# The first norm and modulation of a decoder layer, in four groups by feature chunk

## What is computed

```python
mod = silu(c) @ ada_w + ada_b          # shift1, scale1, gate1, shift2, ... per sequence
h = rmsnorm(x, g1) * (1 + scale1) + shift1
p = h @ w_in                           # queries, keys, values, mLSTM and pool inputs
```

## Time and profile before

| | us |
|---|---|
| three runs of the kernel before | 932.52, 932.40, 927.18; median 932.4 |
| profiled execution, its own time | 932.81 |
| its span in the profile | 931.0 |
| TensorE busy (matmuls) | 845.6 (91%) |
| VectorE, ScalarE, GpSimd busy | 494.6, 348.5, 337.8 |
| chain that ended last | TensorE 73%, of it the product line L687 56% |

### The profile page before, as it was taken

The page is one execution under the profiler, slowest core; times in us unless marked ns, Lnnn a source line. Parts: engine busy times, 40 slices in busy tenths (PEclk is TensorE's granted clock), DMA queues, the critical chain, the costliest instruction groups (busy, mean ns, idle before and its releaser), DMA issues.

```text
span 931.0 us, 19070 instructions
## 1 busy us (share of the span) xinstructions
PE 845.6 (91%) x7555; PEld 750.2 (81%) x7555; DVE 494.6 (53%) x938; ACT 348.5 (37%) x675; POOL 337.8 (36%) x204
## 2 busy tenths in 40 slices
PE   4669999998998688899899699999999999999994
PEld 3458999987556564566699599999999999999994
DVE  0061456565435985667547756666621366667224
ACT  2432222233322133656432355555311355554321
POOL 0133455451000584434324134444344444443440
PEclk9869999999555655999989899999999999999998
DMA  9732788883105772445026123434322333222222
GB/s 346 289 131 73 221 265 261 270 261 129 35 13 179 283 269 41 105 116 154 8 79 254 46 80 114 114 113 115 102 92 91 106 113 121 93 92 90 92 63 92
DMA packets 72438, 128.28 MB, mean 138 GB/s; under 512 B 13652, under 2 KB 48156, under 8 KB 72096
## 3 DMA queue, kind: packets, MB, share of 16 engines
q1 hardware_dynamic: 65664, 109.65, 36.9%
q10 hardware_dynamic: 6656, 17.43, 5.6%
q0 software_dynamic: 32, 0.00, 0.0%
HBM read 121.39 MB, written 9.11 MB: 140 GB/s over the span
## 4 chain that ended last, share of the span: by engine, by line
PE 73%; DVE 13%; SPq 7%; issue 2%; ACT 2%; DMA 1%; POOL 0%; DVEq 0%; ACTq 0%; POOLq 0%
PE ps L687 56%; SPq L490 2%; PE ps L855 2%; PE ps L870 2%; SPq L429 2%; PE ps L744 2%; PE ps L943 1%; PE ps L922 1%; PE ps L907 1%; DVE sq L1354 1%; PE ps L957 1%; SPq L516 1%; DMA arena<-cache_keys 1%; PE ps L737 1%; DVE hR L1362 1%
## 5 line engine op out<-in xcount | busy, mean ns | idle before, releaser
L687 PE MATMUL ps<-hR,wR 128*128 128x260 f32 x3504 | 436.4, 286 | 21.7 <-ACT hR L1051 17.8
L687 PEld LDWEIGHTS ps<-hR,wR 128*128 128x128 f32 x3504 | 429.9, 191 | 27.1 <-issue 19.3
L641 POOL TENSOR_TENSOR wR<-raw,wR 128x1024 fp32r<-128x1024 f32 x95 | 227.7, 2397 | 321.8 <-ACT wR L1043 321.8
L1043 ACT ACTIVATE wR<-raw 128x1024 fp32r<-128x1024 f32 x95 | 100.4, 1058 | 217.8 <-PE ps L687 214.2
L687 PE MATMUL ps<-fR,wR 128*128 128x260 f32 x1056 | 128.1, 283 | 2.2 <-DVE fR L1746 2.0
L687 PEld LDWEIGHTS ps<-fR,wR 128*128 128x128 f32 x1056 | 127.0, 188 | 3.1 <-DVE fR L1746 2.4
L1768 DVE COPY arena<-arena 128x2 f32<-128x2 f32 x44 | 47.1, 1071 | 94.1 <-ACT arena L1301 94.1
L578 POOL TENSOR_TENSOR arena<-arena,par 128x1024 f32<-128x1024 f32 x16 | 33.4, 2089 | 89.8 <-DMA arena<-cache_keys 89.8
L1372 DVE TENSOR_REDUCE arena<-arena 128x64 f32<-128x1024 f32 x16 | 19.5, 1219 | 86.0 <-POOL arena L578 86.0
L1731 DVE TENSOR_TENSOR t<-ps,mod 128x8 f32<-128x8 f32 x24 | 4.0, 166 | 108.8 <-PE ps L687 108.8
L635 POOL TENSOR_SCALAR arena<-arena,fac 128x128 f32<-128x128 f32 (+3 forms) x32 | 40.7, 1274 | 57.2 <-DVE fac L1685 57.1
(11 more groups left out here) (334 smaller groups left out, 994.6 us busy)
## 6 DMA issues: line engine op xcount, KB each, us to landing
raw<-weights SPq DMA_DIRECT2D x95, 512.0 KB, 3.8
arena<-cache_keys SPq DMA_DIRECT2D x128, 192.0 KB, 3.3
arena<-weights SPq DMA_DIRECT2D x24, 512.0 KB, 10.5
arena<-cache_values SPq DMA_DIRECT2D x128, 64.0 KB, 1.9
arena<-weights ACTq DMA_DIRECT2D x12, 512.0 KB, 5.6
raw<-weights ACTq DMA_DIRECT2D x12, 512.0 KB, 4.8
x<-xT SPq DMA_DIRECT2D x8, 260.0 KB, 6.3
out_y<-x SPq DMA_DIRECT2D x8, 260.0 KB, 2.2
```

What stands on the lines that cost most here:

```text
L641: nc.gpsimd.tensor_tensor(wR[:, i % 2, 1, :, :], raw[:, g % RAW, :, :], wR[:, i % 2, 0, :, :].bitcast(F32), ALU.subtract).then_inc(lo_read ...
L687: last = mm(ps[:, a + half, 0:TH], wR[:, i % 2, wp, k, :], src[:, hp, j, half * TH:(half + 1) * TH], start=(j == 0 and q == 0), stop=(j == ...
L1043: A(wR[:, i % 2, 0, :, :], raw[:, g % RAW, :, :], ACT.Identity).then_inc(hi_ready, 1)
```

## The change

The 16 modulation items are reordered into four groups; group c holds scale and shift of feature chunks 2c and 2c+1. A group's four items go through TensorE in one go into one PSUM bank, through ScalarE in one copy (`group_read`), and through one set of four turns. Bias, `ab`, sample columns, normings and both halves of hR are then made for two feature chunks at a time. The first two projection items, 16 and 17, run chunk by chunk beside each other between the groups. The squares are added on VectorE, as in the other two norms, and TensorE sums the total once. Slots 16 and 17 are loaded ahead of slots 8 to 15. SyncE waits for two groups before it loads the first cache half, since slots 2 to 7 now lie there. `half_sums(0)` comes behind the norm, `value_products(0)` behind the first two low halves.

```diff
-EARLY_GROUP = [0, 1, 2, 2, 3, 3, 3, 3, 4, 4, 4, 4, 5, 5, 5, 5]
+EARLY_GROUP = [i // 4 for i in range(EARLY)]
...
-    part1 = [("ada", t, KD) for t in range(16)] + [("in", t, KD) for t in range(N_IN)]
+    part1 = [("ada", t + s, KD) for c in range(4) for t in (8 + 2 * c, 2 * c) for s in range(2)] + [("in", t, KD) for t in range(N_IN)]
...
-            for g in range(N_A + RAW):
+            for g in [*range(8), 16, 17, *range(8, 16), *range(18, N_A + RAW)]:
                 load_slot(g)
 
+                if g == 18:
+                    sp.wait_ge(slot_done, 8)
                 if g in (18, 19) or (half >= 2 and half < 2 * NB and g >= half + 22):
                     load_half(half)
                     half += 1
...
             pool.wait_ge(par_landed, 16)
-            value_products(0)
-            half = 1
+            half = 0
...
-                if i == 3 or (7 <= i < N_IN):
+                if i in (2, 3) or (7 <= i < N_IN):
                     value_products(half)
                     half += 1
```

TensorE (`chunk` is the body of the old loop in `product`, for one chunk):

```diff
+            def group_products(c):
+
+                raw_wait(pe, 4 * c)
+                for i in range(4):
+                    for k in range(KD):
+                        last = mm(ps[strips[k % 4], 6 + c % 2, i * P:(i + 1) * P], sc[:, k, :], raw_slot(4 * c + i)[:, k, :],
+                                  start=(k < 4), stop=(k >= 4))
+                last.then_inc(slot_done, 4)
+
+            def group_turns(c):
+
+                pe.wait_ge(evac_act, 4 * c + 4)
+                if c >= 2:
+                    pe.wait_ge(mod_ready, c - 1)
+                for i in range(4):
+                    last = mm(ps[:, 4 + c % 2, 264 + i * 9:273 + i * 9], modw[:, c % 2, i * P:(i + 1) * P], fold[:, 0:9], start=True, stop=True)
+                last.then_inc(group_turned, 1)
...
-            for k in range(KD):
-                norm_sum(k)
             pe.wait_ge(silu_ready, 1)
+            pe.wait_ge(cwT_evac, 1)
+            group_products(0)
+            norm_total(0)
+            pe.wait_ge(root_ready, 1)
+            group_turns(0)
+            group_products(1)
+            group_turns(1)
+            for j in range(2):
+                chunk(16, j)
+                chunk(17, j)
+            group_products(2)
+            for j in range(2, 4):
+                chunk(16, j)
+                chunk(17, j)
+                if j == 2:
+                    group_turns(2)
+            group_products(3)
+            group_turns(3)
+            for j in range(4, KD):
+                chunk(16, j)
+                chunk(17, j)
```

ScalarE, whose event loop then starts at items 16 and 17 (`hi(2)` comes behind item 16's evacuation):

```diff
+            def group_read(c):
+
+                act.wait_ge(slot_done, 4 * c + 4)
+                if c >= 2:
+                    act.wait_ge(group_turned, c - 1)
+                A(modw[:, c % 2, :], ps[:, 6 + c % 2, :], ACT.Identity).then_inc(evac_act, 4)
+
+            def group_high(c):
+
+                act.wait_ge(h_sample, c + 1)
+                A(hR[:, 0, 2 * c:2 * c + 2, S:T], sc2[:, 2 * c:2 * c + 2, 0:NB], ACT.Identity).then_inc(hs_hi, 1)
+                for k in (2 * c, 2 * c + 1):
+                    act.wait_ge(xn_ready, k + 1)
+                    A(hR[:, 0, k, 0:S], sq[:, k % 2, 0:S], ACT.Identity, bias=mod[:, k, 0:1]).then_inc(h_hi, 1)
+
+            group_read(0)
             root(0)
+            group_read(1)
+            group_high(0)
+            hi(0)
+            hi(1)
+            group_high(1)
+            group_read(2)
+            group_high(2)
+            group_read(3)
+            group_high(3)
```

VectorE:

```diff
+            for k in range(1, KD):
+                add_squares(0, k)
+
+            def group_mod(c):
+
+                dve.wait_ge(group_turned, c + 1)
+                new = ps[:, 4 + c % 2, 264:300].rearrange("p (t c) -> p t c", c=9)
+                for i, t in enumerate((8 + 2 * c, 2 * c)):
+                    last = V.tensor_tensor(mod[:, t:t + 2, :], new[:, 2 * i:2 * i + 2, :],
+                                           par_("ada_b", t, t + 2).unsqueeze(2).broadcast_to([P, 2, 9]), ALU.add)
+                last.then_inc(mod_ready, 1)
+                dve.wait_ge(mod_ready, c + 1)
+                two = slice(2 * c, 2 * c + 2)
+                link(V.scalar_tensor_tensor(ab[:, two, :], mod[:, 8 + 2 * c:10 + 2 * c, :], 1.0,
...
+            def group_normed(c):
+
+                two = slice(2 * c, 2 * c + 2)
+                link(V.tensor_tensor(sc2[:, two, 0:NB], x[:, two, S:T], rstd[:, S:T].unsqueeze(1).broadcast_to([P, 2, NB]), ALU.mult))
...
+                for k in (2 * c, 2 * c + 1):
+                    V.scalar_tensor_tensor(sq[:, k % 2, 0:S], x[:, k, 0:S], ab[:, k, 0:1], rstd[:, 0:S], ALU.mult, ALU.mult)\
+                        .then_inc(xn_ready, 1)
...
+            dve.wait_ge(x_landed, 16 * KD)
+            group_mod(0)
             root(0)
+            group_normed(0)
+            for c in range(1, 4):
+                group_mod(c)
+                group_normed(c)
             half_sums(0)
-            dve.wait_ge(turn_evac, 16)
-            dve.wait_ge(x_landed, 16 * KD)
-            normed(0, "g1", 8, 0)
```

More of the change, by code:

```diff
@@ L187, in trunk_kernel @@
         pages = big[:, 17 * T:17 * T + 2 * HALF * 384].rearrange("p (s j n) -> p s j n", s=2, j=HALF)
[L189 removed]
+        early = [arena[:, 0:D], arena[:, D:2 * D]] + [big[:, g * D:(g + 1) * D] for g in (12, 13, 8, 9, 10, 11, 4, 5, 6, 7, 0, 1, 2, 3)]
+        late = [big[:, g * D:(g + 1) * D] for g in range(len(LATE))]
         extra = [arena[:, 4160 + at:4160 + at + D] for at in (1024, 2048, 6144)]
@@ L661, in _, with chunk @@
             PASSES = [(0, 0), (0, 1), (1, 0)]
+            def chunk(n, j):
+                kind, t, chunks = ITEMS[n]
+                a = 2 * (n % 2)
+                g, k = (CHUNK0[n] + j) // KD, (CHUNK0[n] + j) % KD
+                i = SPLIT.index(g)
+                if j == 0 or k == 0:
+                    pe.wait_ge(lo_ready, i + 1)
+                if (kind, t) in (("in", 0), ("out", 0), ("up", 0)):
+                    v = ("in", "out", "up").index(kind)
+                    pe.wait_ge(h_hi, v * KD + j + 1)
+                    pe.wait_ge(h_lo, v * KD + j + 1)
+                if kind in ("down0", "down1") and t == 0:
+                    pe.wait_ge(f_lo, FH * (kind == "down1") + j + 1)
+                src = fR if kind[:4] == "down" else hR
+                for q, (wp, hp) in enumerate(PASSES):
+                    for half in range(2):
+                        last = mm(ps[:, a + half, 0:TH], wR[:, i % 2, wp, k, :], src[:, hp, j, half * TH:(half + 1) * TH],
+                                  start=(j == 0 and q == 0), stop=(j == chunks - 1 and q == 2))
+                if k == KD - 1:
+                    last.then_inc(slot_done, 1)
+                elif j == chunks - 1:
+                    last.then_inc(item_done, 1)
             def product(n):
                 kind, t, chunks = ITEMS[n]
-                a = 2 * (n % 2)
                 if kind == "ada":
@@ L669, in product @@
                     for k in range(KD):
-                        last = mm(ps[strips[k % 4], a, 0:P], sc[:, k, :], raw_slot(n)[:, k, :], start=(k < 4), stop=(k >= 4))
+                        last = mm(ps[strips[k % 4], 2 * (n % 2), 0:P], sc[:, k, :], raw_slot(n)[:, k, :], start=(k < 4), stop=(k >= 4))
                     last.then_inc(slot_done, 1)
@@ L673, in product @@
                 for j in range(chunks):
[L674 to L692 removed]
+                    chunk(n, j)
+            def group_products(c):
[12 more added lines that the diff above has]
+                last.then_inc(group_turned, 1)
             pe.wait_ge(con_landed, 16)
@@ L708, in step @@
                             pe.wait_ge(tokens_evac, TOKEN_ITEMS.index(n - 2) + 1)
-                        if PART1[n - 2][0] == "ada" and PART1[n][0] == "in":
-                            pe.wait_ge(turn_evac, sum(i[0] == "ada" for i in PART1[:n - 1]))
                     if n == N_A + 1:
```

90 lines of the change are left out of this document (34 added, 56 removed).

## The result

| | before | after |
|---|---|---|
| median of six runs each, us | 931.68 (927.18 to 933.14) | 923.39 (920.89 to 924.62) |
| profiled execution, its own time | 932.81 | 923.26 |
| its span | 931.0 | 921.5 |
| first 128x1024 operation behind the sample query starts | 90.35 | 81.30 |

The ratio of the runs is 0.9915 with a 95% interval of 0.9895 to 0.9936. The kernel is faster, by 8.3 us in the medians and 9.5 us in the two profiled spans.

A forecast was written before the change was run, and what follows sets the result against it. TensorE was taken to bound nearly everything, except a start waiting on cache keys, value product, half sums and norm. Profiled 932.81 less 10.0 gives 922.8; runs' median 0.4 lower than profiled gives 922.4, said as 922.5; range 915 to 930.5.

The forecast's parts named there:

- The root: End of the first norm's sums: ready at 24.9 us against the old 24.83; adds on VectorE bring and cost nothing.
- The low halves: GpSimd's lo(0) and lo(1) hold VectorE at ab of group 1, 31.5 to 36.0; path price 0, worst case 6.7 us.
- The hole ahead of item 18: TensorE idle 3.8 us after items 16 and 17 while item 18's weights are made; item 18 starts at 60.7.
- cold start: Items 18 to 20 on TensorE: 1.67 us charged for the lower clock on top of 17.37, bounds 0 and 3.2.
- Group 0: turns to 25.5: First modulation group behind the root: its four turns, at 0.2 us each, end at 25.5 us.
- group 1's products (25.5 to 27.7): TensorE's products of the second modulation group, taken at the full-rate 2.2 us, ending at 27.7 us.
- Rival E: Products still wait for the last group; only old half sums and value product gained, 4.7 us: 927.7; chance 0.05.
- the likeliest case: The whole step-by-step account of the change holds: 922.5 us, own range 919.5 to 926; chance 0.50.
- B, the kinder clock: Clock back during chunk (17,0), 1.4 to 2.0 us less, and not lost in the 3.8 us hole, 1.67 less: 919; chance 0.20.
- C, the lock on the path: GpSimd's value product stalls group 2's norming if the cache half lands late; 2.1 to 6.7 us, 924.5 to 929; chance 0.15.
- D: Interleaved items leave TensorE at 1.2 GHz throughout: 2.4 us gained, 930.0, or slower, up to 938.6; chance 0.10.
- The late slots: Late slots wait for four landings at once, but have 33 us against a median 10.5 from issue to landing: cost 0.

The follow-up runs named there:

- The two moves alone: Kernel before, with only VectorE's half_sums(0) put behind normed(0) and GpSimd's value_products(0) behind the first two low halves: 921.78 us, ratio 0.9916.
- the best version: Changed kernel with all of item 17 behind item 16, first value product held until VectorE's last low, both high halves right behind the root: 915.45 us, ratio 0.9859.
- item 17 behind and no hold: Changed kernel with all of item 17 behind item 16, the first value product not held back: median 918.88 us, ratio 0.9865.
- the kernel with the hold: Changed kernel with all of item 17 behind item 16 and GpSimd's first value product held until VectorE's last low: 917.73 us, ratio 0.986.

## Why the prediction was right, point by point

**The time.** The forecast was 922.5 with a range of 915 to 930.5. The median of 923.39 is 0.9 above it; the profiled execution, 923.26, stands against a sum of 922.8. The gain was forecast as 10.0 us up to item 20's end. The query point shows 9.05.

**Right.** The root was forecast for 24.9 and stood at 24.56; that the adds bring nothing held within 0.3 to 0.5 us when they were taken out. Group 0's weights landed as worked out: its products started at 18.40 (18.3 said). The later groups' products start behind other work and so do not test the rest of that sum. The low halves stood back to back on `ab` of group 1, locked from 32.57 to 37.00 (31.5 to 36.0 said), at no price on the path: group 1's two lows were done at 40.49, and TensorE asked for them at 43.63. The hole ahead of item 18 was 3.50 us (3.8 said), and the 144 matmuls took 19.07 (17.37 + 1.67 = 19.04 said). Hole and cold start are the terms worth most to copy: what lay beside item 17 came to lie alone once items 16 and 17 ended together.

**The mis-sized term.** It is the step "Group 0: turns to 25.5" and "group 1's products (25.5 to 27.7)". The products ended at 29.15 instead of 27.7, 1.5 us late: 1.1 in the products, 0.7 in the turns, less the 0.3 by which the root was early. The products I sized at full rate, and the clock fell under them (0.64, 0.50, 0.50 in 25 to 28 us): 3.33 instead of 2.2, where the same products took 1.95 at a clock of 1.00. With the turns most of the error is a misread row. I took 0.2 us for each, but a turn leaves two records, and the earlier trace rows give 0.39 for the two. Four turns took 1.28 us here, and still 1.03 at a clock of 1.00 in the run with the squares on TensorE, where 0.6 was said. Of the 1.5 us, 0.5 came back by hi(0), because ScalarE's high part of group 0 took 1.4 us and not 1.8. What follows hangs in a row on this read:

| step | said | measured | late |
|---|---|---|---|
| chunk (16,0) | 33.7 | 34.70 | 1.0 |
| products(2) start | 40.2 | 41.22 | 1.0 |
| turns(3) end | 50.0 | 51.36 | 1.4 |
| last low ends | 54.7 | 55.64 | 0.9 |
| item 18 starts | 60.7 | 61.61 | 0.9 |
| query point, ahead of 90.35 | 10.0 | 9.05 | 0.95 |

The turns of group 3 repeat the misread row: 1.06 us at a clock of 1.00 where 0.7 was left for them, so 1.4 late. VectorE's group 3 took 4.17 us instead of 4.6 and gave that back. This account is argued from the rows; no run warmed group 1's products and left all else as it was. In the run with the squares on TensorE they were warm, but the root and the turns ahead of them came later, and they ended at 29.55.

**Where the reading was wrong, though the time was right.** Rival E priced the old half sums and value product at 4.7 us, from 44.65 to 49.35. The two moves alone gained 9.33. The 4.7 us was the stretch from the low half's start to the norm's; what counts is the stretch from where the norm could have started, 39.36 behind the last turn, to 49.35, less the lock, plus a clock that doesn't fall (1.51 us, which the moves are not shown to bring). In the old trace it was to be read as VectorE's idle time ahead of `half_sums(0)`, from the last turn on. So rival E's time would have been 932.81 - 9.33 = 923.5 for the profiled execution, within a microsecond of the likeliest case, and the two could not be told apart by the time. Only the experiments did: the groups, adds and interleaving brought nothing beside the two moves (81.30 and 81.10 against 81.02).

**The other rivals.** B, the kinder clock, did not come: the clock stayed at 0.50 through the first chunks, until 42 us, and read 0.50 again in 63 to 65 us behind the hole. But the row that I held against it, a pause of 1.5 us being enough to bring the clock to 0.50, is no rule: behind a pause of 1.56 us it stayed at 1.00 in the run with the two moves. C, the lock on the path, did not come in the changed kernel, since the cache half landed at 41.7 and GpSimd's value product ran while VectorE was idle (41.74 to 43.80; `ab` of group 2 is later than 46). Its price was right as a mechanism: 2.14, 1.6 and 0.7 us in the runs where one GpSimd operation did lie there, about 2.1 at most, as said. The Trainium skill ("SBUF — State Buffer", Who interferes with whom) has the block as exclusive for VectorE instructions with two SBUF inputs; the rows agree for `ab`, the sample operations, normings and lows, and the two modulation adds with one input in PSUM took their 0.13 each in all groups, also in group 1, where they stand beside the low half (32.27, beside 32.31). D did not come: the clock was at 1.00 from 43 us to the hole, in the midst of the interleaved chunks.

**Rest.** The late slots cost nothing: from item 20 on the distances between the two kernels' milestones stay between 9.05 and 9.8 us, and the two ends of the spans lie 9.5 apart. One sum of the chances is off by a hundredth: 0.31 and 0.20 are 0.51, where 0.52 was written.

## What to carry to other kernels

Where engines work strictly in order, look first for an operation that stands in the queue ahead of critical work and waits for something unrelated; moving it may bring all that a restructuring promises. Count the gain from the time at which the work behind it could have started, not from when its neighbour did. Two items that end together leave nothing to hide the next item's preparation behind: let one of them end early, even if the engine could interleave them.

## What the runs showed of the hardware that I had not expected

The lock has a grain: of two back-to-back GpSimd operations each holds one VectorE operation until it ends. That one gets through, and the next is held by the second GpSimd operation (2.12 and 2.28 in the changed kernel, 1.95 and 2.28 in the best version; 1.99, 2.73 and 2.54 for three in a row). It works the other way too: GpSimd's low half took 2.87 instead of 2.36 where a VectorE norming had started 0.08 us ahead of it (40.29, 0.74 us).

The granted clock fell while TensorE was at work: from 25 us on it was busy in full, with turns and the 128-column products of a group, and the clock read 0.64, then 0.50. Ahead of that it had worked from 18.40 to 23.10 and stood idle for 1.51 us, to 24.61. Of the kernel before, show such products at full rate. And the clock row does not show every slow stretch: behind an idle time of 8.80 us, group 0's products took 3.62 us with the row at 1.00, as in the kernel before the first sums took 1.23 us for two records against 0.60 later. The length of the records tells it there, not the clock row.

Runs of one kernel spread over 3 to 8 us, in one case 12, and the traces place this. From the query point to the end of the cache keys (which stands at about 220 us) all kernels but one take 134.1 to 134.9 us. The exception is the profiled execution with item 17 behind and no hold, with 141.1: its time, 927.31, is the highest of its runs. Of the 6.3 us, some 4 stand as longer waits of GpSimd for cache keys (54.8 us, and 50.6 in the kernel with the hold); the rest is not placed. In the middle part, from about 294 to 462 us, the profiled executions differ by up to 4 us in a stretch in which the kernels are alike, and behind it by 1.2 at most. A change at the start of this kernel is thus seen at its own point within a few tenths (81.30 and 81.10 in two traces of the changed kernel), and in the total only through that noise.
